# One kernel, its first block rewritten: projections, attention, group norms and half the output product in one sequence of ticks

## The reference

```python
# first block
h = rms_norm(x, norm_mix_pre)
qa, ka, va, qb, kb, vb = split(h @ w_in)          # 8+8 query heads, 2+2 key/value heads of width 64
qa, ka = rope(rms_norm(qa), ang_axial), rope(rms_norm(ka), ang_axial)    # norm per head
out_a = global_attention(qa, ka, va)              # all 512 keys, softmax in float32
qb, kb = rope(qb, ang_1d), rope(kb, ang_1d)
out_b = window_attention(qb, kb, vb, sink)        # |key - query| <= 128, and a sink term in the softmax
mixed = concat(rms_norm(out_a, group_norm_a), rms_norm(out_b, group_norm_b)) @ w_out
x = x + rms_norm(mixed, norm_mix_post)
h = rms_norm(x, norm_ffn_pre)
x = x + rms_norm((silu(h @ w_gate) * (h @ w_up)) @ w_down, norm_ffn_post)   # d_ff = 2816
# second block: causal attention of 8 heads with forget gates, a multiscale pooling branch,
# output product, the same kind of gated feed-forward, a final rms_norm
```

## Time and profile before

| | |
|---|---|
| median of three runs | 1245.6 us |
| the profiled execution | 1246.25 us, span 1244.5 us, mean granted clock of TensorE 0.973 |
| busy in the span | PE 1188.4 us (95%), DVE 658.2, ACT 504.2, POOL 92.5 |
| start to the first sum of squares | 0 to 24.7 us |
| projections | 24.7 to 93 us |
| attention of the first block | 93.7 to 224 us |
| output product of the first block | 224 to 271.5 us (a first part of it interleaved) |
| feed-forward of the first block | 280 to 650 us |
| second block | 650 to 1244.5 us, of it the attention 763 to 821 us |

### The profile page before, as it was taken

How to read it: one execution, slowest core, us unless ns; L and a number is a source line. 1 busy time by engine, 2 the same in 40 slices (tenths; PEclk the granted TensorE clock), 3 DMA queues, 4 the chain that set the end, 5 groups by cost and what they waited for, 6 DMA issues and landing times.

```text
span 1244.5 us, 14874 instructions
## 1 busy us (share of the span) xinstructions
PE 1188.4 (95%) x5262; PEld 931.6 (75%) x5262; DVE 658.2 (53%) x1040; ACT 504.2 (41%) x830; POOL 92.5 (7%) x124
## 2 busy tenths in 40 slices
PE   6979999979999999999997999999999999999996
PEld 4766666767888888888866786777888888888884
DVE  6776767567544444433339776637444444443332
ACT  6765777434333232322224365625333232332221
POOL 0022323003000000000003001300000000000001
PEclk9996999999999999999998998999999999999998
DMA  6220000030422222323320322003232232232211
GB/s 250 101 69 33 1 1 1 3 134 17 135 101 88 97 95 90 101 102 103 105 105 24 111 98 71 1 1 135 72 115 93 93 100 87 100 102 102 101 51 67
DMA packets 28968, 101.32 MB, mean 81 GB/s; under 512 B 3328, under 2 KB 3968, under 8 KB 28800
## 3 DMA queue, kind: packets, MB, share of 16 engines
q1 hardware_dynamic: 28784, 100.53, 23.5%
q10 hardware_dynamic: 144, 0.26, 0.1%
HBM read 98.68 MB, written 2.10 MB: 81 GB/s over the span
## 4 chain that ended last, share of the span: by engine, by line
PE 87%; DVE 7%; ACT 4%; issue 1%; DMA 0%; POOL 0%; DVEq 0%; SPq 0%; ACTq 0%
PE bank L365 24%; PE bank L364 24%; PE bank L363 24%; PE bank L749 7%; PE bank L764 3%; DVE hl L912 2%; PE bank L779 1%; PE bank L780 1%; PE bank L781 1%; DVE ta L904 1%; DVE xres L906 1%; ACT sw L610 1%; ACT wh L271 1%; DVE wl L279 1%; DVE ta L486 1%
## 5 line engine op out<-in xcount | busy, mean ns | idle before, releaser
L363 PE MATMUL bank<-hh,wh 128*128 128x512 f32 x936 | 372.2, 398 | 26.5 <-DVE hl L912 26.2
L279 DVE TENSOR_TENSOR wl<-raw,wh 128x1024 fp32r<-128x1024 f32 x181 | 222.4, 1229 | 327.3 <-ACT wh L271 326.9
L271 ACT ACTIVATE wh<-raw 128x1024 fp32r<-128x1024 f32 x175 | 185.1, 1058 | 466.2 <-PE bank L365 325.4
L364 PE MATMUL bank<-hl,wh 128*128 128x512 f32 x936 | 366.7, 392 | 0.0
L365 PE MATMUL bank<-hh,wl 128*128 128x512 f32 x936 | 366.6, 392 | 0.0
L363 PEld LDWEIGHTS bank<-hh,wh 128*128 128x128 f32 x936 | 177.1, 189 | 71.0 <-issue 24.2
L364 PEld LDWEIGHTS bank<-hl,wh 128*128 128x128 f32 x936 | 177.2, 189 | 38.5 <-issue 2.2
L365 PEld LDWEIGHTS bank<-hh,wl 128*128 128x128 f32 x936 | 177.0, 189 | 37.3
L365 PE MATMUL bank<-gh,wl 128*128 128x512 f32 x352 | 140.4, 399 | 0.0
L364 PE MATMUL bank<-gl,wh 128*128 128x512 f32 x352 | 138.7, 394 | 0.0
L363 PE MATMUL bank<-gh,wh 128*128 128x512 f32 x352 | 138.0, 392 | 0.0
(11 more groups left out here) (168 smaller groups left out, 1251.6 us busy)
## 6 DMA issues: line engine op xcount, KB each, us to landing
raw<-weights SPq DMA_DIRECT2D x181, 512.0 KB, 3.2
xres<-x_t SPq DMA_DIRECT2D x4, 512.0 KB, 8.5
out_t<-final SPq DMA_DIRECT2D x8, 256.0 KB, 2.3
rope<-angles SPq DMA_DIRECT2D x1, 1024.0 KB, 11.4
wp<-pool_weights ACTq DMA_DIRECT2D x1, 256.0 KB, 3.4
mats_raw<-matrices SPq DMA_DIRECT2D x1, 128.0 KB, 9.5
ones<-matrices SPq DMA_DIRECT2D x1, 64.0 KB, 9.6
ident<-matrices SPq DMA_DIRECT2D x1, 64.0 KB, 9.5
```

What stands on the lines that cost most here:

```text
L271: act.activation(wh[:, j, :, :], raw[:, j, :, :], ACT.Copy).then_inc(high_split, 1)
L279: v.tensor_tensor(wl[:, j, :, :], raw[:, j, :, :], wh[:, j, :, :].bitcast(F32), ALU.subtract)\
L363: pe.matmul(bank[:, :], wh[:, slot, b, :], ah[:, k, :], start=first and n == 0, stop=False)
L364: pe.matmul(bank[:, :], wh[:, slot, b, :], al[:, k, :], start=False, stop=False)
```

## The change

1. **Tiles of the projections** come in another order (v tiles in between), and only the first five are projected ahead. The other seven are cut into 56 pieces of one block (three matmuls each) that are dealt out over ticks 0 to 43 of the attention.
2. **Ticks.** A tick is a slot of the attention. `pe_tick`, `vec_tick`, `act_tick`, `gpsimd_tick` and SP's loop each hold what an engine does in a tick, from tables (`END`, `COS`, `SIN`, `DONE`, `PARTS`, ...).
3. **Stacked attention** in both blocks: q's high and low part on 128 partitions, k's high and k's low part each doubled to 128 rows. Scores are two matmuls of 128 rows. v's high and low part lie side by side, so the values are two matmuls with 128 output rows; ACT copies the lower 64 rows out and DVE adds the upper 64 to them. For this each q tile takes two high copies on ACT and two low subtractions on DVE (64x512), each k tile four and four.
4. **Rotation** of the first block moves to POOL (three or four operations of 128x512 a tile); the gains of the head norms are multiplied into the angles beforehand. The **swap** is made by four transfers from `ta` to `sw` a tile, issued by SP.
5. **Head order** becomes `ffffffwwffwwwwww`; scores rotate over two banks, since projections take the other two; three instead of four heads of probabilities are held; the reciprocals are taken once a head, POOL divides two steps' worth a tick.
6. **Group norms**: POOL squares and adds, and scales group A. The heads' outputs are kept in `xres`, so x is loaded a second time (4 transfers) before the residual is added.
7. **Output product**: for its first four tiles the half that needs group A (16 pieces) is dealt out over ticks 60 to 71; the rest follows group B's norm.

```diff
-IN1 = [("norm_rope", "k", 0)] + [("norm_rope", "q", i) for i in range(4)] \
-    + [("rope", "k", 1)] + [("rope", "q", 4 + i) for i in range(4)] + [("v", "v", i) for i in range(2)]
+IN1 = [("norm_rope", "k", 0), ("norm_rope", "q", 0), ("v", "v", 0), ("norm_rope", "q", 1), ("norm_rope", "q", 2),
+       ("rope", "k", 1), ("rope", "q", 4), ("norm_rope", "q", 3), ("v", "v", 1)] + [("rope", "q", i) for i in (5, 6, 7)]
...
+for _p in range(KT * (len(IN1) - 5)):
+    PIECES.setdefault(_p * 44 // 56, []).append((5 + _p // KT, _p % KT))
...
+        def pe_tick(pe, t):
+            if 0 <= t < STEPS:
+                pe_scores1(pe, t)
+            for m in MIDDLE:
+                if MIDDLE[m] == t:
+                    pe_middle1(pe, m)
+            if 0 <= t - TURN < STEPS:
+                pe_turn1(pe, t - TURN)
+            if 0 <= t - VALUES < STEPS:
+                pe_values1(pe, t - VALUES)
+            for m, k in PIECES.get(t, ()):
...
+                ins = products(pe, bank1(m), m % RING, [k], hh, hl, k, k == 0, k == KT - 1)
...
+                products(pe, banks[d], (CHUNK0["out1"] + d) % RING, [k], mix_h[0], mix_l[0], k, k == 0, False)
...
+        def pe_scores1(pe, n):
+            if n < 2:
+                pe.wait_ge(bank_read, 3 + n)
+            else:
+                pe.wait_ge(at1.maxed, n - 1)
             if j == 0:
+                pe.wait_ge(f1.part.low, max(parted(tile1("q", qt)), parted(tile1("k", kt))))
+            bank = banks[2 + n % 2]
+            q = q1[:, Q_ORDER.index(qt) % 4, par, block]
+            todo = [(o, q, kh1[kt][:, par, keys]), (o, q, kl1[kt][:, par, keys])]
...
+            vs = v1[:, vt, kb, par, :, :].rearrange("p a d -> p (a d)")
+            pe.matmul(o, vs, pth[:, n % PT, q0 * P:q1_ * P], start=kb == 0, stop=False, skip_group_check=True)
+            pe.matmul(o, vs, ptl[:, n % PT, q0 * P:q1_ * P], start=False, stop=kb == QB - 1, skip_group_check=True)
...
+        def gpsimd_tick(g, t):
+            if 4 <= t < STEPS + 2 and t % 4 < 2:
+                s = t // 4 - 1
+                for j in (2 * (t % 4), 2 * (t % 4) + 1):
...
+                    g.wait_ge(at1.inverted, s + 1)
+                    g.tensor_scalar(p, p, rden[:, n % 8:n % 8 + 1], 1.0, ALU.mult, ALU.mult).then_inc(at1.normed, 1)
+            for m in ROPED:
+                if t == COS[m]:
+                    if before1(m) is not None:
+                        g.wait_ge(f1.part.low, parted(before1(m)))
+                    g.tensor_tensor(tb[:, r, :], ta[:, r, :], cos, ALU.mult).then_inc(f1.cosined, 1)
+                if t == SIN[m]:
+                    g.wait_ge(f1.swapped[r], 64 * (ROPED.index(m) // 2 + 1))
+                    link(g, "g", g.tensor_tensor(sw[:, r, :], sw[:, r, :], sin, ALU.mult))
+                    g.tensor_tensor(tb[:, r, :], tb[:, r, :], sw[:, r, :], ALU.add)
+                if normed and t == DONE[m]:
+                    g.tensor_tensor(tb[:, r, :], tb[:, r, :], hsq[:, idx % 2, :], ALU.mult).then_inc(f1.done, 1)
...
+        def sync_swap(sp, m):
+            for q in range(4):
+                a, b = q * HALF, (q ^ 1) * HALF
+                sp.dma_start(sw[a:a + HALF, r, :], ta[b:b + HALF, r, :]).then_inc(f1.swapped[r], 16)
...
+            pe.matmul(o, q, in2.kh[par][:, kt, keys], start=True, stop=False)
+            pe.matmul(o, q, in2.kl[par][:, kt, keys], start=False, stop=False)
...
+                    v.wait_ge(at2.lower, s + 1)
+                    v.tensor_tensor(o, banks[6 + s % 2][0:HD, :], o, ALU.add).then_inc(at2.added, 1)
```

More of the change, by code:

```diff
@@ new lines, in ring_free @@
+        def ring_free(pe, what, x):
+            n = RING_USES.index((what, x))
+            if n >= 2:
+                last, y = RING_USES[n - 2]
+                if last == "sum":
+                    pe.wait_ge((n_x, n_ga)[y].ready, 1)
+                elif last == "turn":
+                    pe.wait_ge(at1.pt.low, y + 1)
+                elif y in NORMED:
+                    pe.wait_ge(f1.logged, NORMED.index(y) + 1)
+                else:
+                    pe.wait_ge(f1.part.low, parted(y))
@@ new lines, in act_part1 @@
+        def act_part1(act, m):
+            what, i = IN1[m][1:]
+            if what == "v":
+                act.wait_ge(f1.middle, middle_count(m))
+                act.activation(v1[:, i, :, :, 0, :], ring_bank("middle", m)[:, :].rearrange("p (b h d) -> p b h d", b=QB, h=2),
+                               ACT.Copy).then_inc(f1.part.high, 1)
+                return
+            act.wait_ge(f1.done, done_count(m))
+            src = tb[:, slot1(m), :]
+            if what == "q":
+                n = Q_ORDER.index(i)
+                if n >= 4:
+                    act.wait_ge(at1.scores, 4 * head_at(Q_ORDER[n - 4], 1) + 4)
+                for par, own, other in pair():
+                    ins = act.activation(q1[own, n % 4, par, :], src[own], ACT.Copy)
+            else:
+                for par, own, other in pair():
+                    for rows in (own, other):
+                        ins = act.activation(kh1[i][rows, par, :], src[own], ACT.Copy)
+            ins.then_inc(f1.part.high, 1)
```

1016 lines of the change are left out of this document (619 added, 397 removed).

## The result

The changed kernel takes 1238.58 us (median of 6 runs, 1237.54 to 1238.76), the kernel before 1244.34 (6 runs): ratio 0.9953, 95% interval 0.9940 to 0.9966. That is 5.8 us faster where I had forecast 26: the direction was right, the size was not. The profiled execution took 1238.51 us, its span 1236.7.

What follows compares the result with a forecast made beforehand. PE, busy for 95% of the span, was taken as the bound. From the profiled 1246.25 us, 21.4 us (first block) and 5 us (second) gave 1219.9, or 1219 as a median; range 1199 to 1244 us for 8 in 10.

Steps and rivals of the forecast that it cites:

- The start: Before tick 7, POOL's rotation and divisions set the length: first scores at 48 us, step 0's transposes at 65.5 us.
- What a step loses: PE's attention steps in the first block: a full step falls from 2.18 to 1.44 us, a windowed one from 1.67 to 1.17.
- Ticks 7 to 43: First attention with projection pieces: PE bounds with 85 us of work against DVE's 72; 92 us long with the additions.
- 4 us for unevenness: Allowance in ticks 7 to 43 for DVE's work falling unevenly over the ticks, such as four low parts in tick 9.
- Ticks 44 to 59: First attention without projection pieces: DVE bounds with 28 us of work, against 21 us on PE.
- Ticks 60 on: Last attention ticks, group B's norm and the output product: from 185.5 us to the sum of squares at 252 us.
- the milestone: Sum-of-squares matmul after the first block's output product, at 273.31 us before: forecast near 252 us, 21.4 us earlier.
- Second block: Second attention: PE falls to 4.8 us a head, DVE at 5.3 us now bounds; 5 us gained, bounds 0 and 11.
- Clock: Idling before tick 7 lowers PE's granted clock again: 3 us lost in ticks 7 to 43, between 0 and 13.
- Rival C: PE stays at half clock through half of the interleaved ticks: 1257 us, slower; chance 0.12.
- A: POOL's two-input operations hold DVE's, some 8 us in ticks 7 to 43 and 6 in 44 to 59: 1233 us; chance 0.24.
- D: The cost of changing row counts stays (+15), the second block gives nothing (+5), with a little DVE hold: 1243 us; chance 0.05.

Runs made afterwards that it cites:

- x3: The changed kernel with POOL's rotation and head-norm products cut to 16 of 512 columns, so the rotation is left out of the computation: 1227.46 us.
- x9: The changed kernel with operations moved to later ticks or slots in both attentions, three weight splits moved, first attention's DVE low part in its old tick: 1223.25 us.
- x13: x9 with POOL's rotation of the 7th, 8th, 10th and 12th tile begun at ticks 14, 22, 34 and 46 instead of 12, 19, 31 and 44: 1220.84 us.
- x4: The changed kernel with POOL's rotation of the fifth tile at ticks 5 to 7 instead of 1 to 3, its parts at tick 8: 1245.40 us.
- x6b: The changed kernel with DVE's low part of the transposed probabilities one tick later in the first attention alone: 1252.29 us.
- x12: x9 with POOL's rotation and head-norm products cut to 16 of 512 columns, left out of the computation: 1213.60 us.
- x7b: The changed kernel with rotation and head-norm products on DVE at POOL's ticks; POOL keeps divisions and squares: 1246.51 us.
- x10: x9 with the last two projection tiles' pieces spread over ticks 31 to 50 instead of 31 to 43, the last tile's parts one tick sooner: 1226.28 us.
- x5b: The changed kernel with DVE's low part of the transposed probabilities one slot later in the second attention alone: 1244.88 us.
- x8b: The changed kernel with operations moved to later ticks or slots in both attentions, DVE's low part included in both, and three weight splits moved: 1232.04 us.
- x14: x9 with each of POOL's 35 two-input rotation and head-norm operations replaced by two one-input ones, rotation left out of the computation: 1229.14 us.

## Why the prediction was wrong

- *The start*: tick 7 at 65.4 us, step 0's transposes at 67.2, forecast 65.5 for both; first scores 50.4 for 48. Right in size, partly by luck: the first scores were 2.4 us late, and the stretch behind them 2.4 shorter than forecast. That POOL sets it was half right: without POOL's work it is only 3.4 us shorter (x3), and the hold on DVE's splits, which the forecast leaves out here, is part of that.
- *What a step loses*: right. A full step with one piece takes 74.78 - 72.71 = 2.07 us, so 1.38 without the piece (forecast 1.44), against 2.18; the changing between 64 and 128 rows went:

```profile
72.71 0.40 PE L837 MATMUL bank<-kh,q 128*128 128x512 f32 x1
72.95 0.40 PE L837 MATMUL bank<-kl,q 128*128 128x512 f32 x1
73.19 0.60 PE L847 MATMUL bank<-ident,pr 128*128 128x128 f32 x4
73.54 0.48 PE L863 MATMUL bank<-pth,v 128*128 128x512 f32 x1
...
74.78 0.40 PE L837 MATMUL bank<-kh,q 128*128 128x512 f32 x1
```

- *Ticks 7 to 43, the failed step*: "I add 4 us for unevenness". The busy times were right (84.0 and 73.1 us), but PE idled for 13.8 us where I had set 4, and 3 for the clock: my length was 5.8 us too short. I summed each engine's work and took the larger sum as the length. What stood in its place are waits in the engines' fixed order: x9 and x13 shorten the stretch by 2.4 and 5.2 us with the same work, x4 and x6b lengthen it by 9.9 and 11.8. (My own terms add to 86 us, not 85.)
- *Ticks 44 to 59, failed likewise*: "DVE bounds", 28 us. DVE was busy for only 25.7 of 35.3 us, PE for 22.2: 7.3 us too short. x13 takes 32.0 with the same work.
- *Ticks 60 on*: forecast 66.5 us to the milestone, measured 66.8. Right, though one term was miscounted: two thirds of 16 steps at 1.17 us are 12.5, not 10.4.
- *Second block, failed*: "DVE comes to 5.3 and now bounds". Neither did: of 57.7 us DVE was busy for 44.2 and PE for 46.4. Handovers set the length; by my estimate a ring of 6.0 us a head, hidden just under PE's 6.15. The room was larger than my 5 us: 9.7, shown by x9; the changed kernel's order takes none of it.
- *Clock*: 1.00 in ticks 7 to 43. Rival C fell; my 3 us of loss there were not needed. The half level is gone from 88 to 115 us, but comes back at about 47 to 55, 177 to 181, 197 to 205 and 225 to 233 us; of these the forecast has only the last.
- *Rivals A and D* had totals (1233 and 1243 us) nearer to the measured 1238.6 than mine. D was right that the second block gives nothing and wrong on the row counts. A's hold was to cost 8 us in ticks 7 to 43; DVE lost at most 2.3 us there (x12), and POOL's queue and the order around it are the larger part. Of the 3.4 us at the start, where DVE lost 4.1 us, A may have a share. The Trainium skill, "GPSIMD Engine Reference", Key points, says that VectorE is about twice as fast for elementwise work and that the two contend where VectorE reads two inputs from SBUF. The traces agree with both (1.27 against 0.69 us for such an operation, and the held splits); as a rule for where to put the rotation it would have misled, since x7b, which moves it to DVE, is 7.9 us slower.

My terms were short by 5.8 + 7.3 + 5 us, and 1.5 elsewhere (0.3 from tick 60 on; about 1 because the profiled execution stood 0.65 over the median before and not after): 19.6. Open stays which ring or burst each part of PE's remaining idle time in x13 (9.5 and 9.0 us) comes from, how much of the start is the hold, and whether work for PE in ticks 44 to 59 would fill its idle time if its tile came in time (x10).

## What to carry to other kernels

A stretch in which several engines hand work to each other in every step can be much longer than the work of its busiest engine (here 97.8 us for 84.0, and 57.7 for 46.4): rings of handovers and bursts in one engine's list set it. Before counting a gain from PE's work, follow one step round all engines and add durations and handovers. An instruction whose input comes from another engine in the same step is a candidate for a step later, behind what others wait for. Try all such moves of a ring together, since one alone can lose what both together gain (x5b +6 us, x9 -9.7), and do not take slack from the ring that feeds the bottleneck (x6b +18.5 us, and +6.9 even beside the other moves, x8b against x9).

## What the runs showed of the hardware

POOL and DVE hold each other, and how much depends on the inputs. A weight split on DVE (128x1024, two inputs from SBUF) took 1.22 us at the median of the five before 60 us where POOL had no rotation of full width (x3, x7b), 1.39 beside POOL operations with one SBUF input (x14) and 2.16 beside those with two (changed kernel). DVE's products of 0.69 us were held to more than twice that (3.34 us for two, x4).

The other way round, a POOL operation with one SBUF input of 128x512 took 0.69 to 0.70 us at the median in x14, wherever it wrote. Means of a group mislead here (engine, line, busy us, mean ns):

```profile
L1078 POOL TENSOR_SCALAR tb<-ta,cols 128x512 f32<-128x512 f32 x10 | 9.4, 937 | 19.1 <-DVE ta L959 15.0 <-DVE kl L975 4.2
L1084 POOL TENSOR_SCALAR tb<-tb,cols 128x512 f32<-128x512 f32 x10 | 7.0, 696 | 0.9
```

The first group's mean comes from a few instructions. The longest ran beside two weight splits (timeline of x14):

```profile
31.02 2.62 DVE L360 TENSOR_TENSOR wl<-raw,wh 128x1024 fp32r<-128x1024 f32 x2
31.41 2.71 POOL L1078 TENSOR_SCALAR tb<-ta,cols 128x512 f32<-128x512 f32 x1
```

A two-input POOL operation took 1.27 us at its shortest and 1.29 at the median (changed kernel, rotation), where the earlier trace rows give 1.55 in the mean.
